# Weight conversions, modulation rows and small steps moved in a fused two-block transformer kernel

## The reference

```python
# MLA layer, 8 heads
q = (rms_norm(q_lat, q_a_norm) @ w_uq).reshape(B, S, 8, 192)
kv = (rms_norm(kv_lat, kv_a_norm) @ w_ukv).reshape(B, S, 8, 256)
q, k = rms_norm(q, q_head_norm), rms_norm(k, k_head_norm)    # then rope on 64 of 192
o = causal_softmax_attention(q, k, v, 1.0 / math.sqrt(192))
x = x + (o * silu(gate)) @ w_out
# second block: six modulation vectors from the conditioning vector
m = silu(cvec) @ w_mod + b_mod
h = modulate(rmsnorm(x, norm1_g), sh1, sc1)
q, k, v, hy_in, cf_in = jnp.split(h @ w_in, splits, axis=-1)
attn = neighbourhood_attention(q, k, v, k_ctx, v_ctx, rpb)   # 8 heads, 256 window keys + 256 context keys
hy = hyena_mixer(hy_in, ...)                                  # z <- x_n * (fftconv(z) + D_n z), twice
cf = conformer_conv(cf_in, ...)                               # 31 taps, layer norm, silu
x = x + g1 * (jnp.concatenate([attn, hy, cf], -1) @ w_out)
# expert choice: every expert takes its 32 best tokens
aff = softmax(h2 @ w_router); gate, idx = lax.top_k(swapaxes(aff, 1, 2), 32)
y = (silu(xe @ w1) * (xe @ w3)) @ w2                          # 16 experts, 3 x 8 MB of weights each
```

## Time and profile before

| | |
|---|---|
| median of 3 runs | 1408.07 us (1407.66 to 1408.69) |
| the profiled execution | 1407.66 us, its span 1405.9 us |
| PE busy | 1033.9 us, 74% |
| DVE / ACT / POOL busy | 470.4 / 285.6 / 56.3 us |
| HBM read | 485.22 MB, 346 GB/s over the span |
| granted TensorE clock | 0.890 in the mean |

### The profile page before, as it was taken

How to read it: one execution, slowest core, us unless ns; L and a number is a source line. 1 busy time by engine, 2 the same in 40 slices (tenths; PEclk the granted TensorE clock), 3 DMA queues, 4 the chain that set the end, 5 groups by cost and what they waited for, 6 DMA issues and landing times.

```text
span 1405.9 us, 16134 instructions
## 1 busy us (share of the span) xinstructions
PE 1033.9 (74%) x6966; PEld 564.5 (40%) x6966; DVE 470.4 (33%) x869; ACT 285.6 (20%) x495; POOL 56.3 (4%) x79
## 2 busy tenths in 40 slices
PE   9999999999999996566565655656566465665656
PEld 7877886799978852111111111111111011110113
DVE  5877777787877321010110101101011010110103
ACT  6536665644345210000000000000000000000001
POOL 0005300000000000000000000000000000000000
PEclk9999999999999998786888878888878887888778
DMA  9655169254433899999999999999999999999995
GB/s 378 252 218 197 62 234 366 99 194 178 182 120 144 336 393 428 430 429 429 428 429 431 427 430 429 428 430 428 430 429 429 429 429 429 429 429 429 429 430 217
DMA packets 37343, 487.32 MB, mean 347 GB/s; under 512 B 4279, under 2 KB 5976, under 8 KB 7320
## 3 DMA queue, kind: packets, MB, share of 16 engines
q1 hardware_dynamic: 36152, 484.71, 82.6%
q10 hardware_dynamic: 1120, 1.57, 0.3%
HBM read 485.22 MB, written 1.05 MB: 346 GB/s over the span
## 4 chain that ended last, share of the span: by engine, by line
DMA 49%; PE 36%; DVE 11%; ACT 2%; issue 2%; POOL 1%; DVEq 0%; SPq 0%; ACTq 0%
PE ps L272 34%; DMA ring<-in_expert_w 28%; DMA late<-in_expert_w 10%; DMA few<-in_expert_w 10%; DVE xT L1709 2%; DVE ring_r L326 1%; DMA ring<-in_pieces 1%; DVE V L1677 1%; ACT ring_r L320 1%; DVE U L1677 1%; POOL hT L772 0%; PE ps L1719 0%; DVE ring L588 0%; DVE sm L1376 0%; DVE V L1673 0%
## 5 line engine op out<-in xcount | busy, mean ns | idle before, releaser
L272 PE MATMUL ps<-ring,hT 128*32 128x512 f32 x608 | 101.5, 801 | 78.2 <-DMA ring<-in_expert_w 78.2
L272 PE MATMUL ps<-late_r,ring_r 128*128 128x256 f32 x832 | 153.0, 284 | 4.2 <-DVE U_r L517 2.2
L272 PE MATMUL ps<-ring,G 128*32 128x512 f32 x608 | 100.1, 792 | 76.0 <-DMA ring<-in_expert_w 76.0
L272 PEld LDWEIGHTS ps<-late_r,ring_r 128*128 128x128 f32 x832 | 128.9, 188 | 9.0 <-issue 5.8
L272 PE MATMUL ps<-hT_r,ring_r 128*128 128x256 f32 x400 | 112.6, 282 | 0.0
L326 DVE TENSOR_TENSOR ring_r<-ring,ring_r 128x2048 fp32r<-128x2048 f32 (+1 forms) x44 | 98.7, 2275 | 28.7 <-ACT ring_r L320 28.7
L272 PE MATMUL ps<-U_r,ring_r 128*128 128x256 f32 x480 | 107.0, 283 | 0.4 <-DVE hT_r L505 0.3
L272 PE MATMUL ps<-late,U 128*128 128x256 f32 (+2 forms) x402 | 85.5, 491 | 22.3 <-DVE xT L1709 10.4
L272 PE MATMUL ps<-late,G 128*32 128x512 f32 (+1 forms) x352 | 61.4, 773 | 36.8 <-DMA late<-in_expert_w 36.8
L1726 ACT ACTIVATE late<-ps 128x256 f32<-128x256 f32 x16 | 6.1, 384 | 380.8 <-PE ps L1719 380.8
L320 ACT ACTIVATE ring_r<-ring 128x2048 fp32r<-128x2048 f32 (+1 forms) x44 | 81.9, 1898 | 7.7 <-DMA ring<-in_pieces 6.5
(11 more groups left out here) (329 smaller groups left out, 1239.7 us busy)
## 6 DMA issues: line engine op xcount, KB each, us to landing
ring<-in_expert_w SPq DMA_DIRECT2D x115, 2048.0 KB, 45.9
late<-in_expert_w SPq DMA_DIRECT2D x57, 2048.0 KB, 45.7
ring<-in_pieces SPq DMA_DIRECT2D x20, 2048.0 KB, 8.5
few<-in_expert_w SPq DMA_DIRECT2D x19, 2048.0 KB, 45.4
ring<-in_wmodt SPq DMA_DIRECT2D x8, 2048.0 KB, 8.3
ring<-in_wmodk SPq DMA_DIRECT2D x4, 2048.0 KB, 8.8
ring<-in_pieces SPq DMA_DIRECT2D x2, 1024.0 KB, 7.6
ring<-in_pieces SPq DMA_DIRECT2D x1, 1792.0 KB, 12.0
```

The costliest lines, as they stand in the source:

```text
L272: mm = lambda e, o, l, r, st, sp_=True, sk=False: e.matmul(o, l, r, start=st, stop=sp_, skip_group_check=sk)
```

## The change

- **Two conversions (26, 27)** move ahead of the MLA loop on both engines: on ACT between the square root of the key norms and the eviction of the modulation bank, on DVE behind the scaling of the keys.
- **Modulation row 9**: its first part moves ahead of the key norms, the other three from heads 7 to 10 to steps 1 to 3 of the loop.
- **Softmax of MLA**: the maximum is negated and scaled by two instructions of one column instead of one of two, and so are the reciprocals taken.
- **Conversions 41 to 44, low part** go from DVE (steps 3, 4, 5 and 7 of the attention loop) to POOL: three between the two Hyena additions of round one and round two, one behind round two. ACT's high parts stay.
- **Top-k**: the affinities are copied from PSUM to SBUF once, and the first round reads the copy.
- **Fillers** on PE: 2 to 3 and 0 to 5 in `pe_k_tr`, 10 to 5 ahead of the second scores of the attention stage, (3, 2, 6) to (2, 3, 0) ahead of its output products 4 to 6, 18 to 20 ahead of the slot transposes.

```diff
     def pe_k_tr(e):
         e.wait_ge(s["gate_r"], 6)
-        pe_idle(e, 2, 3)
+        pe_idle(e, 3, 3)
...
             if hp == 1:
-                pe_idle(e, 0, 3)
+                pe_idle(e, 5, 3)
...
-    s8 = lambda h, j, n=1: sm[:, 128 + (h % 4) * 8 + j:128 + (h % 4) * 8 + j + n]
+    s8 = lambda h, j: sm[:, 128 + (h % 4) * 8 + j:129 + (h % 4) * 8 + j]
...
-            e.tensor_reduce(s8(h, t), bank[h % 3][:, a:z], AX.X, ALU.max, negate=True).then_inc(s["ml_mx"], 1)
-        e.wait_ge(s["ml_mx"], 3 * h + 2)
-        e.tensor_tensor(s8(h, 2, 2), s8(h, 0, 2), scq.rearrange("p (t h) -> p h t", t=2)[:, h, :], ALU.mult).then_inc(s["ml_mx"], 1)
+            e.tensor_reduce(s8(h, t), bank[h % 3][:, a:z], AX.X, ALU.max).then_inc(s["ml_mx"], 1)
+            e.wait_ge(s["ml_mx"], 4 * h + 2 * t + 1)
+            e.tensor_scalar(s8(h, 2 + t), s8(h, t), scq[:, 8 * t + h:8 * t + h + 1], -1.0, ALU.mult, ALU.mult).then_inc(s["ml_mx"], 1)
...
-        e.reciprocal(s8(h, 6, 2), s8(h, 4, 2)).then_inc(s["ml_r"], 1)
-        e.wait_ge(s["ml_r"], h + 1)
+        for t in range(2):
+            e.reciprocal(s8(h, 6 + t), s8(h, 4 + t)).then_inc(s["ml_r"], 1)
         for t in range(2):
             a, z = RNG[t]
+            e.wait_ge(s["ml_r"], 2 * h + t + 1)
...
-        pe_idle(e, (0, 0, 0, 0, 3, 2, 6, 0)[i])
+        pe_idle(e, (0, 0, 0, 0, 2, 3, 0, 0)[i])
...
     def dve_top(e):
         e.wait_ge(s["rt_tr"], 1)
+        e.tensor_copy(w0, bank[1][0:16, 0:256]).then_inc(s["rt_top"], 1)
         for r in range(4):
-            src = w0 if r else bank[1][0:16, 0:256]
-            if r:
-                e.wait_ge(s["rt_top"], 2 * r)
-            e.max(m8[:, 8 * r:8 * r + 8], src).then_inc(s["rt_top"], 1)
             e.wait_ge(s["rt_top"], 2 * r + 1)
-            e.match_replace(w0, m8[:, 8 * r:8 * r + 8], src, -1.0).then_inc(s["rt_top"], 1)
...
+            e.max(m8[:, 8 * r:8 * r + 8], w0).then_inc(s["rt_top"], 1)
+            e.wait_ge(s["rt_top"], 2 * r + 2)
+            e.match_replace(w0, m8[:, 8 * r:8 * r + 8], w0, -1.0).then_inc(s["rt_top"], 1)
...
-                pe_idle(e, {1: 10, 3: 3}[i])
+                pe_idle(e, {1: 5, 3: 3}[i])
...
-        pe_idle(e, 18)
+        pe_idle(e, 20)
...
         act_rk(e)
+        conv(28)
         act_mod(e)
...
-            if i in (2, 4, 7, 8):
-                conv({2: 27, 4: 28, 7: 29, 8: 30}[i])
+            if i == 7:
+                conv(29)
+            if i == 8:
+                conv(30)
...
+        dve_mod(e, 9, 0)
         dve_rk(e)
+        conv(28)
         for i in range(11):
...
-            if i in (4, 6):
-                conv({4: 27, 6: 28}[i])
+            if 1 <= i < 4:
+                dve_mod(e, 9, i)
...
-            if 7 <= i:
-                dve_mod(e, 9, i - 7)
...
-            if i in (3, 4, 5, 7):
-                conv({3: 42, 4: 43, 5: 44, 7: 45}[i])
...
         pool_hy_mul(e, 0)
+        e.wait_ge(s["w_lo"], 40)
+        for k in (41, 42, 43):
+            conv_lo(e, k)
         pool_hy_mul(e, 1)
+        conv_lo(e, 44)
```

More of the change, by code:

```diff
@@ L1089, in dve_ml_max @@
             a, z = RNG[t]
-            e.tensor_reduce(s8(h, t), bank[h % 3][:, a:z], AX.X, ALU.max, negate=True).then_inc(s["ml_mx"], 1)
-        e.wait_ge(s["ml_mx"], 3 * h + 2)
-        e.tensor_tensor(s8(h, 2, 2), s8(h, 0, 2), scq.rearrange("p (t h) -> p h t", t=2)[:, h, :], ALU.mult).then_inc(s["ml_mx"], 1)
+            e.tensor_reduce(s8(h, t), bank[h % 3][:, a:z], AX.X, ALU.max).then_inc(s["ml_mx"], 1)
+            e.wait_ge(s["ml_mx"], 4 * h + 2 * t + 1)
+            e.tensor_scalar(s8(h, 2 + t), s8(h, t), scq[:, 8 * t + h:8 * t + h + 1], -1.0, ALU.mult, ALU.mult).then_inc(s["ml_mx"], 1)
     def act_ml_exp(e, h):
-        e.wait_ge(s["ml_mx"], 3 * h + 3)
+        e.wait_ge(s["ml_mx"], 4 * h + 4)
         if h == 0:
@@ L1529, in dve_top @@
         e.wait_ge(s["rt_tr"], 1)
+        e.tensor_copy(w0, bank[1][0:16, 0:256]).then_inc(s["rt_top"], 1)
         for r in range(4):
-            src = w0 if r else bank[1][0:16, 0:256]
-            if r:
-                e.wait_ge(s["rt_top"], 2 * r)
-            e.max(m8[:, 8 * r:8 * r + 8], src).then_inc(s["rt_top"], 1)
             e.wait_ge(s["rt_top"], 2 * r + 1)
-            e.match_replace(w0, m8[:, 8 * r:8 * r + 8], src, -1.0).then_inc(s["rt_top"], 1)
-        e.wait_ge(s["rt_top"], 8)
+            e.max(m8[:, 8 * r:8 * r + 8], w0).then_inc(s["rt_top"], 1)
+            e.wait_ge(s["rt_top"], 2 * r + 2)
+            e.match_replace(w0, m8[:, 8 * r:8 * r + 8], w0, -1.0).then_inc(s["rt_top"], 1)
+        e.wait_ge(s["rt_top"], 9)
         e.tensor_scalar(sel, w0, -1.0, None, ALU.is_equal).then_inc(s["rt_top"], 1)
-        e.wait_ge(s["rt_top"], 9)
+        e.wait_ge(s["rt_top"], 10)
         e.tensor_tensor_scan(slot, sel, sel, 0.0, ALU.add, ALU.bypass).then_inc(s["rt_top"], 1)
-        e.wait_ge(s["rt_top"], 10)
+        e.wait_ge(s["rt_top"], 11)
         e.tensor_tensor(slot, slot, sel, ALU.mult).then_inc(s["rt_top"], 1)
     def pe_slot_tr(e):
-        e.wait_ge(s["rt_top"], 11)
+        e.wait_ge(s["rt_top"], 12)
         for t in range(2):
```

## The result

Measured: 1419.23 us median for the changed kernel (1417.05 to 1420.56, 5 runs) against 1407.69 for the kernel before (1407.40 to 1408.69, 5 runs, the three from above among them): ratio 1.0078, 95% interval 1.0062 to 1.0092. Forecast was 1416.3. The profiled execution took 1419.62 us, its span 1417.8.

The account below looks back on a forecast made before the run. The end was taken as bound by the expert-weight DMA stream, shifting one for one with PE reaching the first expert. MLA 1.7, attention 6.5 and router 0.4 gave 8.6 on 1407.66: 1416.3 us, range 1409.5 to 1421.

Parts of the forecast that it names:

- the part named as the cause: Attention stage: each POOL conversion of 41 to 44 shuts out DVE's SBUF instructions for its whole length; stage +6.5 us.
- POOL's price: Attention stage: one two-input conversion of 2048 columns on POOL takes 4.5 us.
- Where the waits fall: Attention stage: DVE waits at a norm (cost 0), the Hyena gate, the conformer's scaling and its gate; last maximum 7.9 late.
- The last wait: Attention stage: conversion 44 takes the port between the halves of the conformer's gate and costs 4.6 us.
- Fillers: Attention stage: five fewer ahead of the second scores give -0.95 us, six fewer ahead of the output projection 1.4.
- Attention, sum: Attention stage: DVE's waits less the gains from fillers and moved conversions, +6.5 us in all.
- rival 3: Attention stage: the clock falls after PE stands still until about 449.6 us, adding 2.7, to 1419.0 us; chance 0.16.
- MLA: MLA stage: last product gated 3.0 late, less 1.3 for a modulation row no longer ahead of the splits: +1.7 us.
- ACT's early conversions: MLA stage: two weight conversions, 3.7 us together, ahead of ACT's key copies help make the first DVE maximum 3.1 late.
- Router: Router: a PSUM copy ahead of eight dependent DVE steps costs +0.4 us; two more fillers stay hidden.
- Rivals 1, 2 and 4: No mutual exclusion (1406.4 us, chance 0.13); DVE slips in first (1413.7, 0.16); no exclusion plus ACT's delay covered (1404.7, 0.05).

Follow-up runs that it names:

- e1: The changed kernel with conversions 41 to 44 back on DVE, the rest of the change kept: 1408.70 us, ratio 1.0001.
- e2: The kernel before with only conversions 41 to 44 moved to POOL: 1418.95 us, ratio 1.0070.
- e4: The changed kernel with 29 fillers added in four of PE's waits in the attention stage, to hold the clock: 1418.81 us, ratio 1.0072.
- e10: The kernel of e4 measured again, on one chip with e9: 1417.36 us, ratio 1.0061.
- e9: The changed kernel measured again without any edit: 1419.45 us, ratio 1.0073.
- e5: The kernel before with only modulation row 9 moved early: 1408.82 us, ratio 1.0002.
- e6: The kernel before with only conversions 26 and 27 moved ahead of the MLA loop: 1408.63 us, ratio 1.0000.
- e3: The changed kernel with each POOL conversion issued as eight instructions of 128x256 instead of one: 1409.41 us, ratio 1.0007.
- e12: The kernel of e11 with conversions 41 and 42 on POOL in eight pieces each, 43 and 44 on DVE: 1402.15 us, ratio 0.9953.
- e11: The kernel before with row 9 early, ACT conversions rescheduled and fewer PE fillers, including one ahead of each of the last two MLA products: 1402.69 us, ratio 0.9957.
- e8: The changed kernel with POOL's four conversions replaced by memsets that write the same area without reading: 1408.43 us, ratio 1.0002.

## Why the prediction came out as it did

- **Direction and cause: right.** The chance of slower was 0.82, and the part named as the cause is the cause (e1, e2).
- **POOL's price: right.** 4.5 us from the slope of the earlier trace rows; 4.51 to 4.57 measured.
- **Where the waits fall: right.** The norm, the Hyena gate, the conformer's scaling and its gate were the four rows. Counted from the first maximum of the stage (396.67, 3.46 later than before), the maxima came 2.77, 4.87, 3.20 and 7.52 late; the prediction had 2.75, 5.0, 3.2 and 7.9. The last wait was taken at 4.6; it was 4.73 - 0.41 = 4.32.
- **Fillers: the first right, the second a quarter too large.** -0.92 instead of -0.95 at step 1, and -1.05 instead of -1.4 for the six (e1: 1.96 in all).
- **Attention, sum.** Forecast +6.5. With the clock held it was 6.4 (e4, e10), with its falls 8.94 and 8.38. That 6.5 and 6.4 lie so close is in part luck: the wait of the last maximum and the gain from the six fillers were both taken some 0.3 too large, and cancel.
- **The step that failed: the clock.** The forecast took no fall; rival 3 did, at 1419.0 with a chance of 0.16, and the median is 1419.23. The place was right: what the kernel lost to the clock lay behind the 4.05 us, 2.5 us in this trace and 1.5 in e9. The price of 2.7 was near for the first, but the prediction gives no row for it: it takes 5.5 us at half the clock as 2.7 more, and it is the trace of the changed kernel that shows these rows taking half as much again and not twice as long. The sum of rival 3 also lacks the 0.45 of the MLA stage, so the hit to 0.2 is partly luck. Another fall, behind the shorter waits at 425 us, was not foreseen, but cost nothing in this trace: from the first to the seventh maximum it took 42.69 us, and 42.71 in e4. In e9 it cost 0.4. The prediction weighed against a fall that fillers and short products lie on both sides; they did not hold the clock. The rule for the next time: where the sum opens a gap on PE of some 4 us where none was, the rows behind it are priced half as long again in the forecast itself; for waits of about 2 us both cases stay open, since the one ahead of 57.5 us was followed by a fall in six traces of 13.
- **MLA: 0.45 too low (2.15 for 1.7), and for half of the stated reason.** First maximum +2.8 (3.1 forecast), last +3.0 (3.0). The last gate came at 279.68, net of this execution's 1.30, as forecast (279.7); but the 3.0 was taken from 276.67, which is the start of the row behind the gate, and the gate itself began at 276.32 in before. Hence 1.7 instead of 2.15. ACT's early conversions, named first, do move the first maximum, yet the loop gives most of it back: alone they cost 0.48, the rows 1.21 (e5, e6).
- **Router: right.** 0.42 to 0.46 for the copy (0.4).
- **Rivals 1, 2 and 4 fell**: no conversion let such a DVE instruction in before its end.

## What to carry to other kernels

An instruction moved to POOL is priced twice: its own length, and once more as a wait of that length for the next DVE instruction beside it that multiplies or adds two SBUF tensors or scales from SBUF to SBUF; a long one on a stage that DVE paces belongs on DVE or in pieces of the length of a DVE step. A gap of some 4 us that a change opens on PE is priced with the clock behind it; behind one of 2 us the clock fell in some executions and not in others. And for effects under 2 us marks inside the trace (0.02 us repeatable in most stages here, 0.3 in the projections ahead of the attention) tell what medians over executions (3 us of spread) don't.

## What was not expected

- POOL's work grew from 4.51 to some 6.3 us a conversion when it was cut in eight, and yet the loss of 8.94 us in the attention stage was gone: it ended 1.51 ahead of before, 0.45 behind the version with the conversions on DVE (e3, e1). With two of the four placed so it gained 0.99 (e12 against e11).
- A write-only POOL instruction shuts out DVE's one-input scaling (0.49 became 1.66) but not its two-input product (0.42 stayed), and a second POOL instruction right behind the first kept a waiting DVE row out for both (2.98 us, e8).
- The same waits of PE do not always bring the clock down: behind 1.81 and 0.85 us at 425 us it fell to 1.2 GHz in the changed kernel and e9 and not in e2, behind some 2.03 us at 57 us in six traces of 13. The six have their first mark 1.4 us later in the mean than the others, before the change has any part in it.
